# Seven block products instead of eight for the projections, the output projection and the experts, with a ring of four weight matrices

## What is computed

```python
p = h @ w_in                                   # 2048 x 1024 @ 1024 x 6672 columns
# columns A: DeltaNet; B (768): Hyena x0, x1, v; C (768): short conv; G (3072): gates
u = short_conv(p[B], hy_conv_w) + hy_conv_b;  x0, x1, v = split(u);  z = x1 * v
yc = bg * short_conv(cg * hx, sc_conv_w)       # bg, cg, hx = split(p[C])
mix = merged @ w_out                           # 1024 x 1024
x = x + g1 * mix
h2 = rmsnorm(x) * (1 + sc2) + sh2
aff = softmax(h2 @ router_w);  top_val, top_idx = top_k(aff.T, 256)      # 16 experts
xe = h2[top_idx]                               # 256 tokens for each expert
hid = silu(xe @ w_gate[e]) * (xe @ w_up[e])    # 1024 -> 768
x += scatter_add(g2 * (hid @ w_down[e]) * top_val)                        # 768 -> 1024
return rmsnorm(x)
```

## Time and profile before

| | us |
|---|---|
| median of 3 runs (4398.81 to 4404.29) | 4401.27 |
| the profiled execution | 4399.92 |
| its span in the trace | 4398.1 |
| PE busy | 3964.1 |
| DVE busy | 1291.8 |
| ACT busy | 945.5 |
| POOL busy | 670.6 |

### The profile page before, as it was taken

One profiled execution on the slowest core, in us unless ns is written; L12 is line 12 of the kernel. 1 busy time (PEld: TensorE's weight loads), 2 busy tenths in 40 slices (PEclk: granted clock), 3 DMA queues, 4 the chain that ended last, 5 costly groups with the idle time before them and its releaser, 6 DMA issues. The chain is left out here.

```text
span 4398.1 us, 43229 instructions
## 1 busy us (share of the span) xinstructions
PE 3964.1 (90%) x15090; PEld 2406.5 (55%) x15090; DVE 1291.8 (29%) x2443; ACT 945.5 (21%) x2035; POOL 670.6 (15%) x536
## 2 busy tenths in 40 slices
PE   6999997999998997773799999989949999999994
PEld 2444444888884443331344444435537777777773
DVE  4433333655662114323322222212241111111112
ACT  4444452444441010011111111111100000000002
POOL 1112122334430000012011111012210000000000
PEclk9999998999999998896899999999959999999997
DMA  6333312222211003534211111133343445545644
GB/s 246 121 99 101 105 46 67 79 79 81 74 65 48 25 10 104 160 119 143 81 48 53 55 48 61 57 121 139 110 173 111 169 151 205 192 143 190 210 143 173
DMA packets 293868, 484.20 MB, mean 110 GB/s; under 512 B 20940, under 2 KB 171151, under 8 KB 293511
## 3 DMA queue, kind: packets, MB, share of 16 engines
q1 hardware_dynamic: 269618, 417.47, 27.7%
q0 software_dynamic: 12096, 43.86, 3.9%
q10 hardware_dynamic: 12053, 21.56, 1.5%
HBM read 372.05 MB, written 110.77 MB: 110 GB/s over the span
## 5 line engine op out<-in xcount | busy, mean ns | idle before, releaser
L2485 PE MATMUL bank<-xeT,wgu 128*128 128x256 f32 x3072 | 667.2, 380 | 9.9 <-PE bank L2499 9.8
L2485 PEld LDWEIGHTS bank<-xeT,wgu 128*128 128x128 f32 x3072 | 582.4, 190 | 100.9 <-issue 22.1
L627 PE MATMUL bank<-hT,wq 128*128 128x512 f32 x1024 | 449.9, 593 | 0.0
L1360 PE MATMUL bank<-hT,wh 128*128 128x512 f32 x768 | 335.2, 596 | 12.1 <-DMA wh<-in_w_in 9.0
L2499 PE MATMUL bank<-wd,hid_e 128*128 128x512 f32 x768 | 332.3, 592 | 1.5 <-DVE hid_e L2406 1.5
L627 PEld LDWEIGHTS bank<-hT,wq 128*128 128x128 f32 x1024 | 192.5, 190 | 224.8 <-issue 224.2
L1878 PE MATMUL bank<-hT,raw_w 128*128 128x512 f32 x576 | 261.4, 597 | 6.7 <-DMA raw_w<-in_w_in 6.7
L1360 PEld LDWEIGHTS bank<-hT,wh 128*128 128x128 f32 x768 | 145.1, 191 | 195.8 <-issue 195.8
L2136 PE MATMUL bank<-wo,mt 128*128 128x512 f32 x512 | 228.0, 599 | 15.6 <-DMA wo<-in_w_out 15.6
L2499 PEld LDWEIGHTS bank<-wd,hid_e 128*128 128x128 f32 x768 | 144.7, 190 | 177.9 <-issue 177.9
L2427 ACT ACTIVATE sgm<-bank 128x256 f32<-128x256 f32 x96 | 36.9, 384 | 939.5 <-PE bank L2485 939.5
(11 more groups left out here) (349 smaller groups left out, 5260.9 us busy)
## 6 DMA issues: line engine op xcount, KB each, us to landing
wgu<-in_exp_w_gate SPq DMA_DIRECT2D x16, 3072.0 KB, 22.7
wgu<-in_exp_w_up SPq DMA_DIRECT2D x16, 3072.0 KB, 29.7
wd<-in_exp_w_down SPq DMA_DIRECT2D x16, 3072.0 KB, 13.5
ada<-in_ada_w SPq DMA_DIRECT2D x12, 2048.0 KB, 9.9
raw_w<-in_w_in SPq DMA_DIRECT2D x24, 1024.0 KB, 5.4
fa_d<-az ACTq DMA_DIRECT2D x48, 264.0 KB
sp_in<-fa_d SPq DMA_DIRECT2D x66, 192.0 KB, 4.2
kT<-kT_d SPq DMA_DIRECT2D x36, 256.0 KB, 2.9
```

Of the source, the lines that this page charges most:

```text
L627: last = pe.matmul(PS[g % 4][:, 0:width(n)], wq[:, kind, k, :], h_of(k, toff(n), width(n)), start=(k == 0), stop=(k == KD - 1))
L1360: last = pe.matmul(PS[u % 4][:, :], wh[:, kind, k, :], h_of(k, toff(n + 1), TW), start=(k == 0), stop=(k == KD - 1))
L2485: last = pe.matmul(PS[4 + f % 2][:, g * CAP:(g + 1) * CAP], wgu[:, b, g, k, f * P:(f + 1) * P], xeT[:, b, k, :], start=(k == 0), stop=(k = ...
```

## The change

Three stages are rewritten to seven block products for each 2 x 2 block; the loops of the projections and of the experts are written out.

The form is that of the branch merge in all of them: seven products, each over half of the contraction, called p1, p5, u2, C11, u3, C12 and C21 here after what they begin or complete.

**Projections.** 12 quads (2 stretches of 1024 tokens, 6 kinds). Weights come 256 columns (1 MB) at a time into two buffers.

```diff
-            wh = sbt(st, "wh", [P, 6, KD, P])
+            raw, S1, S2, S4 = sbt(st, "raw_h", [P, 2, KD, 2 * P]), *[sbt(st, n, [P, 4, P]) for n in ("S1_h", "S2_h", "S4_h")]
+            T1, T2, T3, T4 = [sbt(st, n, [P, 4, TW]) for n in ("T1_h", "T2_h", "T3_h", "T4_h")]
...
+                    for q in range(NQ):
+                        pe.wait_ge(raw_in[q % 2], 16 * (q // 2 + 1))
+                        if q >= 2:
+                            pe.wait_ge(x_free, q - 1)
+                        product(X(q), w(q, 0, 0), t(p, 0, 0), True).then_inc(p1_mm, 1)
...
+                        product(Z, S1, T1, True).then_inc(p5_mm, 1)
+                        pe.wait_ge(s2_ok, q + 1)
+                        pe.wait_ge(t2_ok, p + 1)
+                        pe.wait_ge(p1s_ok, q + 1)
+                        product(X(q), S2, T2, False).then_inc(u2_mm, 1)
...
+                        product(Y, w(q, 0, 1), t(p, 1, 0), True).then_inc(c11_mm, 1)
...
+                        product(X(q), w(q, 1, 0), T3, False).then_inc(u3_mm, 1)
...
+                        product(Z, S4, t(p, 1, 1), False).then_inc(c12_mm, 1)
...
+                        pe.wait_ge(c22_ok, q + 1)
+                        product(X(q), w(q, 1, 1), T4, False).then_inc(c21_mm, 1)
```

```diff
+                    sp.dma_start(modb[:, :, :].rearrange("p a b -> p (a b)"), mod_d[:, 0:3 * D].to_broadcast([P, 3 * D])).then_inc(mb_in, 16)
                     load_mt(0)
...
+                    weighted(0, 0, b11_ok)
+                    sum1(0)
+                    weighted(0, 1, b12_ok)
...
+                    dve.tensor_tensor(T1[:, :, :], b(0, 1), b(0, 0), ALU.subtract).then_inc(t1_ok, 1)
+                    weighted(1, 0, b21_ok)
+                    sum2(0)
+                    weighted(1, 1, b22_ok)
...
+                    dve.tensor_tensor(T2[:, :, :], b(1, 1), T1[:, :, :], ALU.subtract).then_inc(t2_ok, 1)
+                    sum4(0)
+                    sum3(0)
+                    dve.tensor_tensor(b(0, 1), b(1, 1), b(0, 1), ALU.subtract).then_inc(t3_ok, 1)
...
+                    dve.tensor_tensor(T4[:, :, :], b(1, 0), T2[:, :, :], ALU.subtract).then_inc(t4_ok, 1)
```

**Experts.** Three quads for each of 16 experts, unrolled: gate, up, down. One ring of four buffers of 3 MB holds the matrices in that order:

```diff
+            raw = sbt(st, "raw_e", [P, 4, KD * FF])
...
+                    for n in range(NM):
+                        if n == 3:
+                            sp.wait_ge(slots_ok, 2)
+                        if n >= 4:
+                            sp.wait_ge(c21_mm, n - 3)
...
+                    def into(bank, lhs, rhs, first):
+                        for f in range(HF):
+                            for k in range(4):
+                                fresh = first and f == 0
+                                mm = pe.matmul(bank[:, f * P:(f + 1) * P], lhs[:, k, f * P:(f + 1) * P], rhs[:, k, :], start=fresh and k == 0, stop=k == 3, skip_group_check=not fresh)
+                        return mm
+                    def onto(bank, lhs, rhs, first):
+                        for f in range(HF):
+                            mm = pe.matmul(bank[:, :], lhs[:, f, :], rhs[:, f, :], start=first and f == 0, stop=f == HF - 1, skip_group_check=not first)
+                        return mm
...
+                    for e in range(NE):
+                        gate_or_up(3 * e)
+                        gate_or_up(3 * e + 1)
+                        if e + 1 < NE:
+                            turn(e + 1)
+                        down(3 * e + 2)
...
+                    def gate(e):
+                        n = 3 * e
+                        sum1(n + 1)
+                        sum3(n + 1)
+                        sum2(n + 1)
+                        summed(n, gm[:, 0], Y, y_mm, p1s, p1s_ok, c11_ok)
+                        summed(n, gm[:, 2], X(n), u3_mm, p5s, p5s_ok, c22_ok)
+                        gated(e, 0)
+                        summed(n, gm[:, 1], Z, z_mm, u2s, u2s_ok, c12_ok)
+                        gated(e, 2)
+                        sum4(n + 1)
+                        gated(e, 1)
+                        gated(e, 3)
...
+                    for e in range(NE):
+                        if e + 1 < NE:
+                            token_sums(e + 1)
+                        for j in range(2):
+                            pool.wait_ge(ye_ok, 4 * e + 3 + j)
...
+                        pool.wait_ge(ye_st, 32 * e + 32)
+                        if e + 2 < NE:
+                            gather(e + 2)
```

More of the change, by code:

```diff
@@ L1338, in _, with load_raw @@
                 def _(sp):
[L1339 to L1343, removed]
+                    def load_raw(q):
+                        c0 = B_OFF + quads[q][1] * HW
+                        sp.dma_start(raw[:, q % 2], A["w_in"][0, :, c0:c0 + HW].rearrange("(k p) c -> p k c", p=P)).then_inc(raw_in[q % 2], 16)
@@ L1345, in _, with product @@
+                    for b in range(2):
+                        sp.wait_ge(z_st[b], 64)
                 @block.tensor
                 def _(pe):
-                    def turn(h, n):
-                        pe.wait_ge(z_ok, h * NT + n + 1)
-                        pe.wait_ge(znat_ok, h * NT + n + 1)
+                    def product(bank, lhs, rhs, first):
+                        for k in range(4):
+                            mm = pe.matmul(bank[:, :], lhs[:, k, :], rhs[:, k, :], start=first and k == 0, stop=k == 3, skip_group_check=not first)
+                        return mm
@@ L1407, in _, with kept @@
[L1407 to L1418 removed]
+                    def kept(dst, bank, mm, used, ok, q):
+                        act.wait_ge(mm, q + 1)
+                        if q >= 1:
+                            act.wait_ge(used, q)
+                        act.activation(dst[:, :], bank[:, :], ACT.Copy).then_inc(ok, 1)
@@ new lines, in summed, with product_of @@
+                    def summed(q, i, bank, mm, other, other_ok, ok):
+                        dve.wait_ge(mm, q + 1)
+                        dve.wait_ge(other_ok, q + 1)
+                        if q >= 1 and quads[q - 1][1] in conv_kinds:
+                            dve.wait_ge(post_ok, convs(q - 1, i))
+                        dve.tensor_tensor(summand(q, i), bank[:, :], other[:, :], ALU.add).then_inc(ok, 1)
+                    def product_of(q, i):
+                        if quads[q][1] != 5:
+                            return
+                        if i == 3:
+                            dve.wait_ge(c21_mm, q + 1)
+                        else:
+                            dve.wait_ge((c11_ok, c12_ok, c22_ok)[i], q + 1)
+                        if i < 2:
+                            dve.wait_ge(post_ok, convs(q - 3, 3))
+                        else:
+                            dve.wait_ge(post_ok, convs(q, i - 2))
+                        if i == 3:
+                            dve.wait_ge(x_free, q)
+                        last = dve.tensor_tensor(tmp[:, i % 2, :], cs[:, i, :], summand(q, i), ALU.mult)
+                        last.then_inc(prod_ok, 1)
@@ L2422, in expert @@
-                    def expert(i, b, more):
-                        at = i * 2 + b
-                        for f in range(FT):
-                            act.wait_ge(gu_mm, at * FT + f + 1)
-                            act.wait_ge(gs_ok, at * FT + f + 1)
-                            act.activation(sgm[:, f % 2, :], PS[4 + f % 2][:, 0:CAP], ACT.Sigmoid).then_inc(sg_ok, 1)
-                        if more:
-                            to_sbuf(at + 1, 1 - b)
-                    to_sbuf(0, 0)
```

976 lines of the change are left out of this document (683 added, 293 removed).

## The result

The changed kernel took 4218.15 us (median of 4 runs, 4217.12 to 4221.37), beside 4400.04 us of the kernel before on the same chip (4 runs, 4394.93 to 4404.29): a ratio of 0.9588, 95% interval 0.9572 to 0.9605. The forecast was 4222, with a range of 4205 to 4272. The profiled execution took 4217.12 us, its span is 4215.3.

The account below looks back on a forecast made before the run. Bound by PE's matmul pace in each changed stage. Experts -118.7, projections -43.4, output projection -18.7 and barrier +1.5 sum to -179.3: span 4218.8, time 4222 us, range 4205 to 4272.

Parts of the forecast that it names:

- Record price, 0.1117 us at 128 columns: Experts' gate and up: each 128-column f32 matmul record, with its weight load, starts 0.1117 us after the last.
- Rival A: Experts' gate and up: 128-column records cost more than 0.1117 us; 4530 us at 0.169, about 4455 by skill; chance 5%.
- Experts, -118.7: Experts: seven products instead of eight bring an expert from 64.70 to 57.28 us, 118.7 us less over 16.
- I put nothing in their place: Experts: PE's two loop waits for its own last matmul go with the 64.70 us; no new waits are priced.
- The 49 packets: Experts written out: 49 packets of PE instructions, priced at nothing as fetched ahead, with 59 us as the other end.
- Output, -18.7: Output projection: 27.4 us fewer matmuls, 10.0 us lost at the start, 1.3 us shorter tail, sum -18.7 us.
- barrier +1.5: Extra barrier with semaphore clearing: costs 1.5 us, between ends of 0 and 3.5.
- Projections, -43.4: Hyena and short-conv projections: PE ends 45.1 us earlier, the tail grows 1.7 us, sum -43.4 us.
- ACT's stores go; SP's four stores a half lie behind a load that is not late: Projections: ACT no longer stores, and SP's stores queue behind a load expected on time; 1 us added for waits.
- Rival B: Seven-product quads: C22 not ready for the seventh product, slack 1.8 us; 50 to 80 us lost, 4272 to 4302; chance 14%.
- Rival C: Experts' ring of four weight buffers: loads late, 500 us if each takes 29.8 us one after the other; chance 3%.
- Rival D: Experts as reckoned, output and projections give half: 31 us less gain, 4253 us; chance 15%.

Follow-up runs that it names:

- the kernel with halves: Kernel before, with each 256-column gate and up product in the experts' hardware loop split into two of 128 columns: 4493.99 us (1.0222).
- the unrolled kernel: Kernel before, with PE's and SP's part of the experts written out, eight products kept, PE's waits for its own last matmul removed: 4384.85 us (0.9974).
- One and three sums more: Changed kernel with the first weight sum of every experts quad formed once more, or three times more, before the real one: 4217.95 and 4335.89 us.
- ring of three: Changed kernel with three weight buffers instead of four in the experts, the routing lists in a place of their own: 4218.00 us (0.9595).
- ring of two: Changed kernel with two weight buffers instead of four in the experts, the routing lists in a place of their own: 4378.94 us (0.9956).
- experiments 1 and 2: Kernel before with gate and up products as 128-column halves, in the hardware loop (4493.99 us) and written out (4406.09); eight products unsplit, written out (4384.85).

## Why the prediction was right, and where it was off

- **What bounds.** Right: each stage went by the pace of its matmul records.
- **Record price, 0.1117 us at 128 columns** from the routing lists: right, 0.1117 in the experts and 0.112 in the kernel with halves. Rival A is out. With it goes, for these f32 records, the factor 1.45 between 81 and 56 ns that the Trainium skill ("TensorE: Matmul & The Clock Gate", "Back-to-back issue gap") gives for such pairs: by the prediction's estimate from it, 5376 records would have taken 231 us more.
- **Experts, -118.7**: measured -118.8 from the first gate product to the first transfer of the final norm, 119.1 with the routing and the final norm. "I put nothing in their place" of the loop's waits was right; the unrolled kernel gives their worth as 12.3 us. The 49 packets were priced at nothing, and the page shows 104 in all against 60, with no idle time of PE: right.
- **Output, -18.7 and barrier +1.5**: -18.3 for both, against -17.2. The chain through DVE came out within 0.3 us at each of its steps. The barrier was a little too dear: the kernel with the output projection of before keeps it, and its stage took 288.39 us against 287.2 to 287.7 in the four kernels without it, so about 1 us. Later pairs were 0.3 us longer each than forecast.
- **Projections, -43.4**: measured -36.4. The step that failed is "ACT's stores go; SP's four stores a half lie behind a load that is not late", together with "I add 1 us for waits". The load was not late in landing, but its issue waits for a quad's last product, and the stores stand behind that wait. Two waits of 2.0 us and 1.8 us of slower matmuls after the second make 5.8 instead of 1. The first product took 6.6 us instead of 5.9. The tail, from the end of the last product to the next stage's first transfer, grew from 4.7 us to 1649.62 - 1642.16 = 7.5, by 2.7 instead of 1.7. These three, 4.8, 0.7 and 1.0 us, are 6.5 of the 7.0 that are missing. That the stores' place in SP's order is the cause is read from the trace; a kernel with the stores ahead of the load was not tried.
- **The transform behind the projections, unchanged and priced at nothing**, gave 8.0 us. That made up for the miss, so the total of the first two is -44.4 where -43.4 was forecast: the sum was closer than its terms, by luck, as nothing in the forecast speaks of this stage. By the traces' 182.8 us against the 179.3 forecast, the projections' miss of 7.0 stands against 8.0 here and 2.5 in the other rows. The stage is the subject of the last section.
- **Rival B (C22 late)** at 14% was dearer than it should have been. The slack was read as 1.8 us, the time by which C22 is early, while DVE's idle time ahead of it counts as well: 4.0 us. The rival's 3.4 us more of DVE work would have cost nothing in a gate or up quad and 0.9 us in a down quad (slack 2.5), an estimate of some 14 us in all and not 50 to 80, without what a wait costs behind itself. One and three sums more bear out that the slack is the sum of both times.
- **Rival C (ring late)**: 29.8 us was the landing of three loads together; one by one they land in 10.1 to 16.5. The 24 us of cover of a ring of three is enough, the 5.4 of a ring of two is not.
- **Rival D** (half of the output and projections): its mechanism, the start-up chain, was in the forecast at its right size.

## What to carry to other kernels

Price a product scheme by matmul records at the pace that an unbroken stretch of the same type and width shows, and look for the operations that could be late at the point where PE wants them: the slack is the time by which the result is early plus the idle time of its engine just ahead of it. On a queue that both loads and stores, ask of each store what the load ahead of it waits for. A hardware loop of PE cost no stop with the short body here; when a change makes the body longer, look at the first matmuls after the turn back and at the count of instruction packets.

## What the runs showed that was not expected

**The turn back of a long loop.** 61.8 us of stops in six turns for a body of 896 matmul records, none for 512, and none for either body when written out (experiments 1 and 2); the packets show that only the long one is fetched again. Where between 512 and 896 it begins was not measured.

**A stage that nobody changed took 8 us less.** The first transform of Hyena depends on small loads. Its first 40 us in three kernels, and for the third the next 40 too: before, changed, and changed with the experts of before (windows, columns as above).

```profile
1687.08:1727.08 40.00, 27.48 (x65) 10.56 (x66) 15.95 (x24) 0.00 (x0) 0.00 (x0) 0.76 0.44 133
```
```profile
1649.62:1689.62 40.00, 27.30 (x74) 10.73 (x75) 17.46 (x27) 0.00 (x0) 0.00 (x0) 0.86 0.49 146
```
```profile
1652.26:1692.26 40.00, 25.58 (x64) 9.76 (x64) 15.86 (x24) 0.00 (x0) 0.00 (x0) 0.82 0.44 129
1692.26:1732.26 40.00, 32.80 (x80) 12.51 (x80) 18.95 (x29) 0.00 (x0) 0.00 (x0) 0.83 0.55 166
```

At nearly the same busy time PE did 65 records at a granted clock of 0.76 before, and 74 at 0.86 in the changed kernel; the stage took 131.7 and 123.7 us. In the third kernel the clock stayed at 0.83 for the next 40 us too, and the same code took 134.7 us. Over all traces the five kernels with the projections of before have 128.1 to 131.7 us here; of the nine with the new ones seven have 123.4 to 124.0, and the other two 129.4 and 134.7. So the stage's time goes with the clock that it is granted at its start (0.76 in the first 40 us of all five, 0.86 in the seven, 0.80 and 0.82 in the two), and the new projections ahead of it mostly leave it a better start. The 134.7 is from the longest of that kernel's four runs, so it is a matter of the execution too. Why the start is better, and whether the clock or the landing of the loads comes first, stays open.

**A wait of PE can cost more than its length, by the clock.** After 6.6 us of waiting 24 records took 5.46 us instead of 2.85 (ring of two), and after 2.0 us eight took 5.37 instead of 3.60 (projections). Windows of these two stretches, columns as above:

```profile
3534.79:3540.04 5.25, 5.25 (x24) 5.25 (x25) 3.61 (x5) 0.94 (x2) 0.00 (x0) 0.50 0.02 3
```
```profile
1599.02:1604.23 5.21, 5.21 (x9) 2.19 (x9) 0.00 (x0) 0.35 (x1) 0.00 (x0) 0.67 0.26 78
```

The granted clock was 0.50 in the first, the 1.2 GHz level, and 0.67 on average in the second, where it rose again within the stretch. After the other wait of 2.0 us in the projections it stayed at 1.00, and eight records took 3.67. With three more sums the clock fell after 14 of the 15 waits of 2.8 us (4.25 to 4.51 us for six records instead of 2.74) and not after the waits of 1.1 us (2.92 us for 24). So the waits alone give only a lower bound of what a late operand costs: three more sums showed 70 us of waits for DVE in the experts (39.4 + 16.0 + 14.9) and cost 118.
